# Hybrid attention layer: the smallest tile's top-k by striking out, causal products joined in and grouped, four banks for ten products, sparse PV in one piece

## The chip, the cores and the metric

The kernel runs on one core of a Trainium2 chip. The metric is the device time of one execution in microseconds (us). TensorE is the matrix engine (PE in the profile, with PEld for its weight loads), VectorE is DVE, ScalarE is ACT, GpSimd is POOL, SyncE is SP. A "bank" is one of the 512-column pieces of PSUM, the memory that TensorE writes its products to.

## What is computed

One layer with two attention branches over 16 meta tokens and 512 inputs (528 keys), 8 heads each, width 1024. Cut to what matters here:

```
proj = layer_norm(concat(meta, x)) @ w_in          # qa ka va ga qi ki wi cq ckv kpe gb
# latent branch: q from rms_norm(cq), k and v from rms_norm(ckv), 32 rotary columns, causal softmax
lb = (q_nope @ k_nope + q_pe @ k_pe) * scale_b;  lb = where(causal, lb, NEG);  ob = softmax(lb) @ vb
# sparse branch: an index score picks 128 keys for every query
idx = sum_h relu(qi_h @ ki) * wi_h
idx = where(s_pos < 16, inf, idx);  idx = where(causal, idx, -inf);  sel = top_k(idx, 128)
la = qa @ ka[sel] * scale_a + bias[t5_bucket(distance)];  oa = softmax(la) @ va[sel]
out = concat(oa * silu(ga), ob * silu(gb)) @ w_out;  return layer_norm(ALPHA * h + out)
```

The 16 meta keys are always picked, so the kernel has to find the 112 best of the others (`PICKED = 112`). A query in the first tile of 128 has only 128 others.

## The kernel before

**Tiling.** The 512 queries are four tiles of 128 (i = 0 to 3). Tile i sees `NK[i]` = 144, 272, 400 or 528 keys. Its index scores lie in `iw` in 128 (i + 1) columns. Those of future keys hold -1e38 (`FUTURE`).

**Order.** One list, `ORDER`, is built by `schedule()`. Every engine walks through it and issues what is its own of each stage, so the order on each engine follows the list and engines meet at semaphores. The list's stages that matter here:

- `("J", kind, n, m)`: a product ("job") of TensorE with three passes for each block of weights (high and low parts), which ACT, DVE or both copy out of its bank. Kinds: `gate` (n = 7 is the last), `uv` (values of the latent branch, five row chunks m), `qn`, `kn` (queries, keys of the latent branch for a pair of heads), `va`, `qa`, `ka` (the sparse branch), `out`, and `tq`, three transposes.
- `("TOPK", round, half)`: top-k on DVE. A round is one MAX8 (the 8 largest of a row) and one MATCH_REPLACE8 (these 8 set to `TAKEN`) for each tile; half 0 is tile 3, half 1 tiles 0, 1, 2. There are 14 rounds (`PICKED // 8`), so 28 halves. `pick(n)` puts the next n halves in the list. `MASK` then turns `iw` into the mask.
- `("S", g)`: scores of head g (0 to 7 latent, 8 to 15 sparse), `X` their exponentials on ACT, `R` the reciprocals and the scaling on POOL, `TP` the transposes into the two banks `ps_t`, `("PV", pair, part)` the products with the values for a pair of heads, in `ps_o`: part 0 is key chunk 0 (512 columns for each of two heads), part 1 the four others.
- `QPE`: ACT issues two DMAs that bring a pair's 32 rotary rows into `q_b`; the scores wait for them.

**Banks.** A job j before the last sixteen output products writes bank `j % 2` of `ps_j`. Its first matmul waits until job j - 2 is copied out, by ACT (`job_act`) and, where DVE copies, by DVE (`job_dve`):

```
                    elif j >= 2:
                        pe.wait_ge(job_act, BY_ACT[j - 1])
```

The two banks of `ps_t` hold index scores of odd heads until the last DVE addition (`i_add`), and the transposes from `TP` 0 on.

**The stretch around the last gate.** After the index scores TensorE makes `gate` 6, `uv` 0 and 1, `gate` 7, `uv` 2 and 3, `qn` 0, `kn` 0 (two halves), `uv` 4, `va` 0 (its first chunk) and then the scores of head 0. DVE meanwhile runs seven halves of top-k, copies `qn` 0 (L1001) and both halves of `kn` 0 (L1005), and goes on with three more halves.

**Scores of the latent branch.** For each tile there is one matmul in 4-byte floats (two for tile 3, which crosses a bank), which the trace records as two passes each (L1429), and behind it one bf16 matmul of 144 columns that adds the causal mask through the identity (L1433). Tiles 3, 1, 0 are unit 0, tile 2 is unit 1, and each unit has one semaphore.

**Sparse PV.** For pairs whose PV is `late` (g = 7, 9, 11, 13: four times) part 0 stands ahead of the last job of the stage, and part 1 behind `TP` and `tq`.

## Time and profile before

| | |
|---|---|
| median of 3 runs (lowest to highest) | 351.72 us (350.32 to 351.91) |
| the profiled execution's own time | 351.87 us |
| its span in the trace | 350.0 us |
| TensorE's mean granted clock | 0.992 of 2.4 GHz |
| busy: PE, PEld, DVE, ACT, POOL | 328.1, 272.5, 229.8, 171.9, 184.6 us |

The profile is of one execution. Its span is 1.9 us shorter than that execution's own time. Busy time of an engine is a sum over stages with different limits; matmul ends are modelled, so the starts of neighbouring rows tell more than their durations.

### The profile page before, as it was taken

Reading aid. Unit: us, or ns where it says so; the run is one execution under the profiler, and the core shown is the slowest. Engines: PE = TensorE matmul, PEld = TensorE weight load, DVE = VectorE, ACT = ScalarE, POOL = GpSimd, SP = SyncE. Lnnn points to the kernel's source line nnn. Section 1 sums busy time; section 2 is a strip of 40 time slices with the busy share of each in tenths; the row PEclk is TensorE's granted clock in tenths of the full one; section 3 lists DMA queues with packets and bytes.
Section 4 is the critical chain, followed back from the end, with each engine's and each line's share of the span. In section 5 each row is a group of like instructions: output and inputs, shape, how many; then the busy total and the mean of one; then the engine's idle time right before and its main releaser. Section 6 shows DMA issues by size and latency. Waiting matters only on the chain.

```text
span 350.0 us, 6150 instructions
## 1 busy us (share of the span) xinstructions
PE 328.1 (94%) x2147; PEld 272.5 (78%) x2147; DVE 229.8 (66%) x619; ACT 171.9 (49%) x378; POOL 184.6 (53%) x171
## 2 busy tenths in 40 slices
PE   0699999999999998999999999999999999999990
PEld 0488977788778776888696878788878888998990
DVE  5762220259965899987985985546676865644586
ACT  4664554353442444465443563747767762732211
POOL 4341899959322251354522459397838372460462
PEclk9999999999999999999999999999999999999996
DMA  7464333229422130101400114042323101130023
GB/s 265 172 179 175 120 122 122 90 65 298 143 81 84 60 113 24 62 15 63 136 2 15 62 28 187 11 143 91 93 91 95 61 10 53 60 123 0 2 89 153
DMA packets 11566, 32.87 MB, mean 94 GB/s; under 512 B 2392, under 2 KB 2392, under 8 KB 11536
## 3 DMA queue, kind: packets, MB, share of 16 engines
q1 hardware_dynamic: 8944, 27.08, 22.6%
q10 hardware_dynamic: 2592, 5.40, 5.1%
q8 instruction: 18, 0.29, 0.3%
q14 instruction: 12, 0.10, 0.1%
HBM read 29.83 MB, written 4.81 MB: 99 GB/s over the span
## 4 chain that ended last, share of the span: by engine, by line
PE 80%; DVE 12%; issue 3%; ACT 2%; DMA 2%; SPq 0%; DVEq 0%; ACTq 0%
PE ps_j L1233 47%; PE ps_o L1478 6%; PE ps_s L1429 6%; PE ps_s L1437 3%; PE ps_t L1233 2%; PE ps_j L1275 2%; PE ps_t L1448 2%; DVE iw L1071 2%; DMA res<-in_x 2%; PE ps_s L1399 2%; DVE top L1067 2%; PE ps_t L1453 1%; DVE iw L1055 1%; PE ps_j L1286 1%; PE ps_j L1291 1%
## 5 line engine op out<-in xcount | busy, mean ns | idle before, releaser
L537 POOL TENSOR_TENSOR wl<-raw,wh 128x1024 fp32r<-128x1024 f32 (+2 forms) x33 | 77.3, 2350 | 75.2 <-ACT wh L544 75.1
L1233 PE MATMUL ps_j<-hh,wh 128*128 128x512 f32 (+2 forms) x224 | 79.2, 354 | 0.1
L1233 PE MATMUL ps_j<-hl,wh 128*128 128x512 f32 (+2 forms) x224 | 78.0, 348 | 0.0
L1233 PE MATMUL ps_j<-hh,wl 128*128 128x512 f32 (+2 forms) x224 | 77.7, 347 | 0.0
L667 POOL TENSOR_SCALAR pr<-pr,rden 128x528 f32<-128x528 f32 (+1 forms) x64 | 35.1, 568 | 53.2 <-DVE rden L1113 53.2
L1233 PEld LDWEIGHTS ps_j<-hh,wh 128*128 128x128 f32 (+1 forms) x224 | 41.8, 187 | 10.1 <-issue 4.4
L1233 PEld LDWEIGHTS ps_j<-hh,wl 128*128 128x128 f32 (+1 forms) x224 | 41.8, 187 | 5.5
L1233 PEld LDWEIGHTS ps_j<-hl,wh 128*128 128x128 f32 (+1 forms) x224 | 41.8, 187 | 5.4 <-issue 0.2
L544 ACT ACTIVATE wh<-raw 128x1024 fp32r<-128x1024 f32 (+2 forms) x35 | 36.0, 1040 | 0.2 <-DMA raw<-in_weights 0.2
L1071 DVE MATCH_REPLACE8 iw<-top,iw 128x512 f32<-128x512 f32 (+3 forms) x56 | 26.2, 475 | 0.0
L677 POOL TENSOR_TENSOR bm<-bias,mask 128x144 f32<-128x144 f32 (+3 forms) x32 | 25.4, 827 | 0.0
L1067 DVE MAX8 top<-iw 128x8 f32<-128x512 f32 (+3 forms) x56 | 24.5, 478 | 0.0
L860 ACT ACTIVATE pr<-ps_s,mn 128x528 f32<-128x528 f32 (+3 forms) x32 | 16.9, 539 | 15.0 <-DVE mn L1099 15.0
L1233 PE MATMUL ps_j<-wh,hh 128*128 128x256 f32 (+1 forms) x80 | 22.9, 286 | 0.0
L1233 PE MATMUL ps_j<-wl,hh 128*128 128x256 f32 (+1 forms) x80 | 22.5, 281 | 0.0
L1233 PE MATMUL ps_j<-wh,hl 128*128 128x256 f32 (+1 forms) x80 | 22.4, 280 | 0.0
L1429 PE MATMUL ps_s<-k_b,q_b 96*128 96x240 f32 (+4 forms) x80 | 22.3, 406 | 0.0
L763 ACT ACTIVATE mix<-ps_j 128x512 f32<-128x512 f32 x8 | 4.8, 598 | 33.7 <-PE ps_j L1233 33.7
L860 ACT ACTIVATE pr<-pr,mn 128x528 f32<-128x528 f32 (+3 forms) x32 | 18.0, 567 | 3.5 <-DVE mn L1101 3.4
L1011 DVE TENSOR_TENSOR ks<-ps_j,ks 64x264 fp32r<-64x264 f32 x32 | 13.8, 430 | 8.9 <-ACT ks L793 8.1
L1233 PE MATMUL ps_j<-wh,mbh 128*128 128x256 f32 x64 | 18.5, 288 | 0.3 <-DVE res L1020 0.3
L1233 PE MATMUL ps_j<-wh,mbl 128*128 128x256 f32 x64 | 18.1, 283 | 0.0
(234 smaller groups left out, 785.6 us busy)
## 6 DMA issues: line engine op xcount, KB each, us to landing
raw<-in_weights SPq DMA_DIRECT2D x37, 512.0 KB, 3.4
bias_by_distance<-bias_vector ACTq DMA_DIRECT2D x1, 2624.0 KB, 13.4
bias<-bias_by_distance ACTq DMA_DIRECT2D x8, 264.0 KB, 3.4
res<-in_x SPq DMA_DIRECT2D x4, 512.0 KB, 5.4
out<-res SPq DMA_DIRECT2D x3, 512.0 KB, 2.6
pt<-in_ln_emb_g SPq DMA_DIRECT2D x1, 512.0 KB, 4.8
pt<-in_ln_emb_b SPq DMA_DIRECT2D x1, 512.0 KB, 6.8
q_b<-qpe ACTq DMA_DIRECT2D x8, 64.0 KB, 2.0
```

Source lines behind the costliest of these rows:

```text
L537: eng.tensor_tensor(ring_of(False, b), raw_of(b), ring_of(True, b).bitcast(F32), ALU.subtract).then_inc(done, 1)
L544: act.activation(ring_of(True, b), raw_of(b), ACT.Copy).then_inc(w_high, 1)
L667: pool.tensor_scalar(a, a, rden[:, k, n:n + 1], 1.0, ALU.mult, ALU.mult).then_inc(scaled, 1)
L677: pool.tensor_tensor(bm[:, h % 2, s], bias[:, h % 4, T - NK[i]:T], mask[:, s], ALU.add).then_inc(folded, 1)
L860: act.activation(dst, src, ACT.Exp, bias=mn[:, k, n:n + 1], scale=-1.0, accum_out=den[:, k, n:n + 1]).then_inc(e_done, 1)
L1011: dve.tensor_tensor(ks[HD - HD * v:P - HD * v, e, v, s], bank[HD * e:HD * e + HD, 0:264], ks[HD * v:HD * v + HD, e, v, s].bitcast(F32), AL ...
L1067: dve.max(top8[:, i, :], iw[:, IOFF[i]:IOFF[i] + P * (i + 1)]).then_inc(done, 1)
L1071: dve.match_replace(out=a, in_to_replace=top8[:, i, :], in_values=a, imm_value=TAKEN).then_inc(done, 1)
L1233: last = pe.matmul(dst, a, b, start=n == 0 and part[0], stop=n == count - 1 and part[1])
L1429: pe.matmul(dst, q_b[:, e, i * P:(i + 1) * P], k_b[:, e, a:b], start=True, stop=b <= c0)
L1437: last = pe.matmul(dst, qs[:, p % 2, e, i * P:(i + 1) * P], ks[:, e, v, a:b], start=v == 0, stop=v == 1)
L1478: last = pe.matmul(ps_o[HD * e:HD * e + HD, q0:NQ], v[0:r, j, c:c + HD], pt[0:r, e, CO[j]:CO[j] + NQ - q0], start=j == 0, stop=j == 4)
```

## The change

Five edits:

1. **Striking out.** A new stage `FLIP` writes the negated index scores of tile 0 in reverse column order into a tensor of its own, `drop`. Two rounds on `drop` take away the 16 lowest scores; rounds 3 to 14 leave tile 0 out. `MASK` reads `drop` backwards with the comparison turned round.
2. **Picks.** The pick ahead of `uv` 0 is 4 halves where it was 5, and the pick in stage g = 0 is 2 where it was 1.
3. **Four banks.** The ten jobs from `uv` 0 to `va` 0 (`FRONT`) rotate through four banks, two of `ps_j` and two of `ps_t`. Every job waits for the last job in its own bank (`PRIOR`), the first two in `ps_t` for `i_add`, and `TP` 0 for the last of `FRONT`. Outside `FRONT` the banks are those of before.
4. **Scores of the latent branch.** The causal matmuls stand behind all score matmuls of their unit: three in a row in unit 0, one in unit 1. Tiles 1 and 0 share their banks with the two pieces of tile 3 and start without the flag that begins a group.
5. **Sparse PV.** Both parts of a late pair stand together behind `TP` and `tq`.

```diff
@@ schedule()
     job("qpe", 1)
+    order.append(("FLIP",))
     pick(2)
     job("gate", 6, extra=0)
-    pick(5)
+    pick(4)
     job("uv", 0, 0, extra=0)
...
         if g < HEADS and g % 2 == 0:
-            pick(1 if g == 0 else 2)
+            pick(2)
...
         for n, j in enumerate(jobs):
-            if late and n == len(jobs) - 1:
-                order.append(("PV", pair, 0))
             job(*j, extra=int(j[0] == "out"))
...
         if late:
-            order.append(("PV", pair, 1))
+            order += [("PV", pair, 0), ("PV", pair, 1)]
@@ banks
+FRONT = range(NJ["uv", 0, 0], NJ["va", 0, 0] + 1)
+
+def bank_of(j):
+
+    if j in FRONT:
+        n = (0, 2, 3, 1)[(j - FRONT[0]) % 4]
+        return n if n >= 2 else (FRONT[0] + n) % 2
+    if j >= TAIL:
+        n = (j - TAIL) % 4
+        return n if n >= 2 else (TAIL + n) % 2
+    return j % 2
+
+BANK = [bank_of(j) for j in range(len(JOBS))]
+PRIOR = [max([i for i in range(j) if BANK[i] == BANK[j]], default=None) for j in range(len(JOBS))]
...
-TOPK_HALF = [(3,), (0, 1, 2)]
+DROP_ROUNDS = (P - PICKED) // 8
+TOPK_HALF = [lambda r: (3,), lambda r: (0, 1, 2) if r < DROP_ROUNDS else (1, 2)]
@@ build(), vector
+                elif stage == "FLIP":
+                    dve.wait_ge(i_add, 4 * HEADS)
+                    dve.tensor_scalar(drop_back, iw[:, IOFF[0]:IOFF[0] + P], -1.0, None, ALU.mult).then_inc(flipped, 1)
...
+                        a = iw[:, IOFF[i]:IOFF[i] + P * (i + 1)] if i else drop[:, :]
...
                         dve.tensor_scalar(mask[:, POFF[i] + META:POFF[i] + NK[i]],
-                                          iw[:, IOFF[i]:IOFF[i] + P * (i + 1)], TAKEN, MASKED, ALU.is_gt,
-                                          ALU.mult).then_inc(masked, 1)
+                                          iw[:, IOFF[i]:IOFF[i] + P * (i + 1)] if i else drop_back, TAKEN, MASKED,
+                                          ALU.is_gt if i else ALU.is_le, ALU.mult).then_inc(masked, 1)
@@ build(), tensor
+            def bank_free(j):
+
+                if PRIOR[j] is None and BANK[j] >= 2:
+                    pe.wait_ge(i_add, 4 * HEADS)
+                elif BANK[j] >= 2 and j >= TAIL > PRIOR[j]:
+                    pe.wait_ge(t_act, 2 * HEADS)
+                    pe.wait_ge(t_dve, 2 * HEADS)
+                elif PRIOR[j] is not None:
+                    pe.wait_ge(job_act, BY_ACT[PRIOR[j] + 1])
+                    if BY_DVE[PRIOR[j] + 1]:
+                        pe.wait_ge(job_dve, BY_DVE[PRIOR[j] + 1])
...
                                 if g < HEADS:
-                                    c0 = NK[i] - 144
-                                    pe.matmul(dst, q_b[:, e, i * P:(i + 1) * P], k_b[:, e, a:b], start=True,
-                                              stop=b <= c0)
-                                    if b > c0:
-                                        lo = max(a, c0)
-                                        last = pe.matmul(ps_s[:, SOFF[i] + lo:SOFF[i] + b], identb[:, :],
-                                                         causal[:, lo - c0:b - c0], start=False, stop=True)
+                                    pe.matmul(dst, q_b[:, e, i * P:(i + 1) * P], k_b[:, e, a:b], start=i >= 2,
+                                              stop=b <= NK[i] - 144, skip_group_check=True)
...
+                        if g < HEADS:
+                            for i in tiles:
+                                a = SOFF[i] + NK[i] - 144
+                                last = pe.matmul(ps_s[:, a:a + 144], identb[:, :], causal[:, :], start=False, stop=True,
+                                                 skip_group_check=True)
                         last.then_inc(s_mm, 1)
```

DVE from the third round of top-k to the copies of `qn` 0 and `kn` 0 (`q_b`, `k_b`), before and then of the change:

```order
L1067 MAX top<-iw 128x8 [waits topk_long]
L1071 MATCH_REPLACE iw<-top,iw 128x512 [waits topk_long]
L1067 MAX top<-iw 128x8 [waits topk_short] x3
L1071 MATCH_REPLACE iw<-top,iw 128x128 [waits topk_short]
L1071 MATCH_REPLACE iw<-top,iw 128x256 [waits topk_short]
L1071 MATCH_REPLACE iw<-top,iw 128x384 [waits topk_short]
L1067 MAX top<-iw 128x8 [waits topk_long]
L1071 MATCH_REPLACE iw<-top,iw 128x512 [waits topk_long]
L1001 TENSOR_SCALAR q_b<-ps_j 64x512 [waits job_mm]
L1005 COPY k_b<-ps_j 64x264 [waits job_mm] x2
```

```order
L1092 MAX top<-iw 128x8 [waits topk_long]
L1096 MATCH_REPLACE iw<-top,iw 128x512 [waits topk_long]
L1092 MAX top<-iw 128x8 [waits topk_short] x2
L1096 MATCH_REPLACE iw<-top,iw 128x256 [waits topk_short]
L1096 MATCH_REPLACE iw<-top,iw 128x384 [waits topk_short]
L1020 TENSOR_SCALAR q_b<-ps_t 64x512 [waits job_mm]
L1024 COPY k_b<-ps_t 64x264 [waits job_mm]
L1024 COPY k_b<-ps_j 64x264 [waits job_mm]
L1092 MAX top<-iw 128x8 [waits topk_long]
L1096 MATCH_REPLACE iw<-top,iw 128x512 [waits topk_long]
```

The third round has two tiles in its second half, and the fourth half of tile 3 stands behind the copies; the first two rounds, ahead of this piece, are as long as before, with `FLIP` ahead of them.

TensorE in the same stretch, from `kn` 0 (its two halves) over `uv` 4 to the first matmul of `va` 0, before and then of the change; `ps_j` and `ps_t` tell the bank:

```order
L1233 MATMUL ps_j<-ckh,wh 128x264 [waits job_act,job_dve,w_low,w_high]
L1233 MATMUL ps_j<-ckl,wh 128x264
L1233 MATMUL ps_j<-ckh,wl 128x264
L1233 MATMUL ps_j<-ckh,wh 128x264 [waits job_act,job_dve,w_low,w_high]
L1233 MATMUL ps_j<-ckl,wh 128x264
L1233 MATMUL ps_j<-ckh,wl 128x264
L1233 MATMUL ps_j<-wh,ckh 16x512 [waits job_act,job_dve,w_low,w_high]
L1233 MATMUL ps_j<-wh,ckl 16x512
L1233 MATMUL ps_j<-wl,ckh 16x512
L1233 MATMUL ps_j<-wh,hh 128x256 [waits job_act,job_dve,w_low,w_high]
```

```order
L1258 MATMUL ps_t<-ckh,wh 128x264 [waits job_act,job_dve,w_low,w_high]
L1258 MATMUL ps_t<-ckl,wh 128x264
L1258 MATMUL ps_t<-ckh,wl 128x264
L1258 MATMUL ps_j<-ckh,wh 128x264 [waits job_act,job_dve,w_low,w_high]
L1258 MATMUL ps_j<-ckl,wh 128x264
L1258 MATMUL ps_j<-ckh,wl 128x264
L1258 MATMUL ps_j<-wh,ckh 16x512 [waits job_act,job_dve,w_low,w_high]
L1258 MATMUL ps_j<-wh,ckl 16x512
L1258 MATMUL ps_j<-wl,ckh 16x512
L1258 MATMUL ps_t<-wh,hh 128x256 [waits job_act,job_dve,w_low,w_high]
```

The order is the same. The second half of `kn` 0 waited for the copy of `qn` 0, two jobs back, and now waits for that of `uv` 2, four jobs back; `va` 0 is now the one that waits for the copy of `qn` 0.

TensorE in the scores of a latent head, before and then of the change:

```order
L1429 MATMUL ps_s<-k_b,q_b 128x240 [waits kp,qpe_in,i_add,job_dve,job_act]
L1429 MATMUL ps_s<-k_b,q_b 128x288
L1433 MATMUL ps_s<-causal,identb 128x144
L1429 MATMUL ps_s<-k_b,q_b 128x272
L1433 MATMUL ps_s<-causal,identb 128x144
L1429 MATMUL ps_s<-k_b,q_b 128x144
L1433 MATMUL ps_s<-causal,identb 128x144
L1429 MATMUL ps_s<-k_b,q_b 128x400 [waits i_add]
L1433 MATMUL ps_s<-causal,identb 128x144
```

```order
L1455 MATMUL ps_s<-k_b,q_b 128x240 [waits kp,qpe_in,i_add,job_dve,job_act]
L1455 MATMUL ps_s<-k_b,q_b 128x288
L1455 MATMUL ps_s<-k_b,q_b 128x272
L1455 MATMUL ps_s<-k_b,q_b 128x144
L1464 MATMUL ps_s<-causal,identb 128x144 x3
L1455 MATMUL ps_s<-k_b,q_b 128x400 [waits i_add]
L1464 MATMUL ps_s<-causal,identb 128x144
```

The matmuls are the same nine; two of the three places where a bf16 matmul stood between two 4-byte ones inside unit 0 are gone.

## Rows read from the trace of the kernel before

**Rows 1.** The page: busy time, share of the span, instructions of TensorE; weights made by ACT.

```profile
PE 328.1 (94%) x2147; PEld 272.5 (78%) x2147; DVE 229.8 (66%) x619; ACT 171.9 (49%) x378; POOL 184.6 (53%) x171
...
L544 ACT ACTIVATE wh<-raw 128x1024 fp32r<-128x1024 f32 (+2 forms) x35 | 36.0, 1040 | 0.2 <-DMA raw<-in_weights 0.2
```

**Rows 2.** Busy time in 120 to 140 us, all engines, clock, DMA.

```profile
120.00:140.00 20.00, 18.01 (x91) 13.65 (x90) 19.32 (x65) 9.77 (x15) 6.20 (x11) 1.00 0.26 85
```

**Rows 3.** TensorE in order of time, 120 to 135 us: start, duration, line, shape.

```profile
120.62 0.40 PE L1233 MATMUL ps_j<-wh,ckl 128*128 128x512 f32 x1
120.86 0.40 PE L1233 MATMUL ps_j<-wl,ckh 128*128 128x512 f32 x1
121.44 0.47 PE L1233 MATMUL ps_j<-wh,ckh 128*128 128x512 f32 x1 [0.18 <-ACT mix L763]
121.75 0.40 PE L1233 MATMUL ps_j<-wh,ckl 128*128 128x512 f32 x1
...
131.23 0.28 PE L1233 MATMUL ps_j<-ckh,wl 128*128 128x264 f32 x1
133.13 0.36 PE L1233 MATMUL ps_j<-ckh,wh 128*128 128x264 f32 x1 [1.62 <-DVE q_b L1001]
...
134.04 0.40 PE L1233 MATMUL ps_j<-wl,ckh 128*16 128x512 f32 x1
134.41 0.35 PE L1233 MATMUL ps_j<-wh,hh 128*128 128x256 f32 x1
```

**Rows 4.** DVE in order of time, 120 to 133 us.

```profile
120.14 0.69 DVE L1067 MAX8 top<-iw 128x8 f32<-128x512 f32 x1
...
121.53 1.07 DVE L1067 MAX8 top<-iw 128x8 f32<-128x128 f32 x3
122.52 0.07 DVE L1071 MATCH_VALUE_LOAD iw<-top,iw 128x8 f32 x1
...
122.77 0.08 DVE L1071 MATCH_VALUE_LOAD iw<-top,iw 128x8 f32 x1
...
132.30 0.69 DVE L1001 TENSOR_SCALAR q_b<-ps_j 64x512 f32<-64x512 f32 x1
```

**Rows 5.** Rotary DMAs of head 0: issue, landing of all eight, load for first scores.

```profile
134.49 1.22 ACTq L802 DMA_DIRECT2D q_b<-qpe  x2
...
DMA to landing us min/median/max: 1.9/2.0/3.7
...
137.31 0.30 PEld L1429 LDWEIGHTS ps_s<-k_b,q_b 96*128 96x128 f32 x2
```

**Rows 6.** TensorE in the scores of head 5, and causal weight loads of all heads.

```profile
181.53 1.05 PE L1429 MATMUL ps_s<-k_b,q_b 96*128 96x240 f32 x4
182.42 0.23 PE L1433 MATMUL ps_s<-causal,identb 128*128 128x144 bf16 x1
...
183.06 0.46 PE L1429 MATMUL ps_s<-k_b,q_b 96*128 96x144 f32 x2
183.35 0.23 PE L1433 MATMUL ps_s<-causal,identb 128*128 128x144 bf16 x1
183.42 0.88 PE L1429 MATMUL ps_s<-k_b,q_b 96*128 96x400 f32 x2
...
L1433 PEld LDWEIGHTS ps_s<-causal,identb 128*128 128x128 bf16 x32 | 3.1, 98 | 1.9
```

**Rows 7.** Chain that ended last, by start and duration, 232 to 298 us.

```profile
232.38 2.91 PE ps_j L1233 x24
235.29 1.01 PE ps_o L1478 x4
236.30 3.12 PE ps_j L1233 x24
...
240.87 1.75 PE ps_o L1478 x16
...
295.81 2.60 PE ps_o L1478 x20
```

More of the change, by code:

```diff
@@ L300, with topk_count @@
 LAST_IN_JOB = max(n for n, j in enumerate(JOBS) if j[0] not in ("out", "tq"))
-TOPK_HALF = [(3,), (0, 1, 2)]
+DROP_ROUNDS = (P - PICKED) // 8
+TOPK_HALF = [lambda r: (3,), lambda r: (0, 1, 2) if r < DROP_ROUNDS else (1, 2)]
+def topk_count(r, half):
+    return 2 * sum(len(TOPK_HALF[half](n)) for n in range(r))
 def build(nc, x, meta, ln_emb_g, ln_emb_b, rel_bias, ln_post_g, ln_post_b, weights, gains, onehot, cos_t,
@@ L340, in build @@
         wi = sb("wi", [P, QT, HEADS])
+        drop = sb("drop", [P, P])
         top8 = sb("top8", [P, QT, 8])
@@ L466, in build @@
         centred = sem("centred")
+        flipped = sem("flipped")
         squared = sem("squared")
@@ L481, in job_bank @@
         def job_bank(j):
-            if tail_bank(j) in (2, 3):
-                return ps_t[:, 512 * tail_bank(j) - 1024:512 * tail_bank(j) - 512]
-            return ps_j[:, (TAIL + tail_bank(j)) % 2 if j >= TAIL else j % 2, :]
+            if BANK[j] >= 2:
+                return ps_t[:, 512 * BANK[j] - 1024:512 * BANK[j] - 512]
+            return ps_j[:, BANK[j], :]
         def vec_bank(n):
@@ L1060, in _ @@
                     r, half = arg
-                    tiles, done = TOPK_HALF[half], topk[half]
+                    tiles, done = TOPK_HALF[half](r), topk[half]
                     if r == 0:
                         dve.wait_ge(i_add, 4 * HEADS)
+                        dve.wait_ge(flipped, 1)
                     for n, i in enumerate(tiles):
+                        a = iw[:, IOFF[i]:IOFF[i] + P * (i + 1)] if i else drop[:, :]
                         if r:
-                            dve.wait_ge(done, len(tiles) * (2 * r - 1) + n + 1)
-                        dve.max(top8[:, i, :], iw[:, IOFF[i]:IOFF[i] + P * (i + 1)]).then_inc(done, 1)
+                            last = TOPK_HALF[half](r - 1)
+                            dve.wait_ge(done, topk_count(r, half) - len(last) + last.index(i) + 1)
+                        dve.max(top8[:, i, :], a).then_inc(done, 1)
                     for n, i in enumerate(tiles):
-                        a = iw[:, IOFF[i]:IOFF[i] + P * (i + 1)]
-                        dve.wait_ge(done, len(tiles) * 2 * r + n + 1)
+                        a = iw[:, IOFF[i]:IOFF[i] + P * (i + 1)] if i else drop[:, :]
+                        dve.wait_ge(done, topk_count(r, half) + n + 1)
                         dve.match_replace(out=a, in_to_replace=top8[:, i, :], in_values=a,
@@ L1074, in _ @@
                     for half in range(2):
-                        dve.wait_ge(topk[half], 2 * len(TOPK_HALF[half]) * ROUNDS)
+                        dve.wait_ge(topk[half], topk_count(ROUNDS, half))
                     for i in range(QT):
                         dve.tensor_scalar(mask[:, POFF[i] + META:POFF[i] + NK[i]],
-                                          iw[:, IOFF[i]:IOFF[i] + P * (i + 1)], TAKEN, MASKED, ALU.is_gt,
-                                          ALU.mult).then_inc(masked, 1)
+                                          iw[:, IOFF[i]:IOFF[i] + P * (i + 1)] if i else drop_back, TAKEN, MASKED,
+                                          ALU.is_gt if i else ALU.is_le, ALU.mult).then_inc(masked, 1)
                     dve.wait_ge(masked, QT)
@@ L1262, in _ @@
                     low_made(pe, NB["out", n])
[L1263 to L1264 removed]
+                    bank_free(j)
                     output_part(n, 0, 0, 3)
@@ L1446, in _ @@
                         pe.wait_ge(t_act, g)
+                    else:
+                        pe.wait_ge(job_act, BY_ACT[FRONT[-1] + 1])
+                        pe.wait_ge(job_dve, BY_DVE[FRONT[-1] + 1])
                     for i in range(QT):
```

18 lines of the change are left out of this document (3 added, 15 removed).

## The prediction

> **What bounds the kernel now.** I read the page first, for which engine is full. TensorE is busy 94% of the span, the next engine 66% [rows 1]. So only two things can shorten this program: taking idle time away from TensorE, or taking work away from it. I then looked for where TensorE is not full, in the table by stretches. It is idle for 22 us in all (350.0 less 328.1), most of them ahead of the first products and behind the last ones, which the change doesn't touch. Of the stretches in between, 120 to 140 us loses most: TensorE has 18.01 of 20 us there, and DVE 19.32 [rows 2]. TensorE's order of time in that stretch shows four gaps [rows 3]. The reader should look at the distance between starts, not at the idle time in brackets, because the modelled ends overlap. Last I read the two places where TensorE changes from one kind of work to another: the scores of a latent head [rows 6] and the late PV [rows 7].
>
> **Four banks and striking out: the gaps.** Two 512-column products in a row start 0.24 us apart (120.62, 120.86). The next starts 0.58 us later, so 0.34 is lost, and the one after it is 0.31 behind instead of 0.24, another 0.07 [rows 3]. That is 0.41 us for `uv` 1, which waits for the copy of `gate` 6 out of the bank two jobs back. The same gap stands once more, at `uv` 3: two, 0.82 us. The third is the big one. The second half of `kn` 0 starts 1.90 us after the last matmul of the first; 264 columns at that rate take 0.12, so 1.78 is lost, and 0.07 behind it, 1.85. Its releaser is DVE's copy of `qn` 0. The fourth, ahead of `va` 0, is 0.37 less 0.24 and 0.07, 0.20 us. Sum of all four: 2.87 us.
>
> With four banks `uv` 1 and `gate` 7 need only the last index addition, long done, and `uv` 3 waits for `uv` 0. `kn` 0 waits for `gate` 7 and `uv` 2. So the first three gaps go. What waits now for the copy of `qn` 0 is `va` 0, and this is where the top-k edit matters. TensorE would reach it at 134.41 - 2.87 = 131.54.
>
> When is that copy made? Before, DVE goes from 120.14 to 132.30, three rounds and one more half of tile 3 in 12.16 us [rows 4]. A half of tile 3 is 121.53 - 120.14 = 1.39, so a round is 3.59. Tile 0's part of a round: its value load and replacement take 122.77 - 122.52 = 0.25, and its MAX8 some 0.20 of the 0.99 that three take for 128, 256 and 384 columns (by columns alone a sixth, 0.17). So 0.45 us a round, 12 rounds of them saved, 5.4 us of DVE in all. Of these only one falls ahead of the copy, and the moved half counts more. After: `FLIP`, two whole rounds 7.18, one half of 1.39, one of 3.59 - 1.39 - 0.45 = 1.75. `FLIP` isn't in the trace. Its nearest rows are 128 columns of MAX8 by share, 0.17, below, and the 512-column copy of `q_b`, 0.69, above [rows 4]; I take 0.25, what value load and replacement of the same 128 columns need. The copy starts at 120.14 + 0.25 + 7.18 + 1.39 + 1.75 = 130.71 and ends at 131.40. TensorE started 0.14 after it before (132.99 to 133.13), so `va` 0 may start at 131.54: exactly when TensorE gets there. The gaps are all gone, with nothing to spare: at a `FLIP` of 0.69 us, 0.44 comes back.
>
> **What is late next.** Behind `va` 0 come the first scores. They need the rotary rows of head 0, whose two DMAs ACT issues at 134.49 in 1.22 us together, when `uv` 4 is done. The second goes off near 135.1 and lands a median 2.0 us later, at 137.1; the first load for the scores is at 137.31 [rows 5]. The distance from `uv` 4 to the scores shrinks by the fourth gap, 0.20, so the load would be due at 137.11 on the old clock and waits some 0.1 us. If it lands after 3.7 us, the longest of the eight, the wait is 1.7. I take 0.1. Front: 2.87 - 0.1 = 2.8 us. From there everything, weight loading too, moves up with TensorE; ACT waited for raw weights 0.2 us in the whole program [rows 1], so I charge nothing for them, and at most that if their cover goes.
>
> The rest of the saved DVE time lies beside a full TensorE and is worth nothing.
>
> **Scores of the latent heads.** 528 columns in 4-byte floats take 182.42 - 181.53 = 0.89 us, 1.69 ns a column; 144 would take 0.24 but take 183.35 - 183.06 = 0.29 behind a causal product. The causal product itself holds the array for 0.07 (183.35 to 183.42) [rows 6]. So each change back from bf16 to 4-byte costs about 0.05, three inside a head's scores. Grouping leaves one: 0.10 saved. Against that, the second and third causal product in a row can no longer hide their weight load behind a long matmul. The record of such a load is 98 ns [rows 6]. If it sets the pace, each costs 0.03 more, 0.06, and 0.04 is left; if it is hidden too, 0.10. I take the middle, 0.07, times 8 heads: 0.56 us, between 0.3 and 0.8. If load and product follow each other with no overlap, it is 2 x 0.10 - 0.10 = 0.10 lost a head, 0.8 us in all. Leaving out the flag that begins a group on tiles 1 and 0 costs nothing: same matmuls, same columns.
>
> A rule of the Trainium skill speaks against this edit. "TensorE: Matmul & The Clock Gate", section on LDWEIGHTS, gives a load of 128 columns 107 ns whatever the contraction, and its section on back-to-back gaps some 81 ns for a load and a 128-column product in a stream. By the first, grouping would be worth about 0.03 a head, 0.2 us in all; by the second about 0.08, 0.6 us. The case's row has 98 ns for the load and no two causal products in a row.
>
> **Sparse PV in one piece.** In the chain the first part takes 1.01 us and the second 1.75; in one piece ten matmuls of the same kind take 2.60. The job between the parts takes 3.12 where its twin takes 2.91, because TensorE has to come back to it [rows 7]. So 1.01 + 1.75 + 0.21 - 2.60 = 0.37 us, four times: 1.5 us. The end of the PV stays where it was against the next scores, so ACT's and DVE's copies behind it see the same distance, and the copies of the last `ka` get 1 us more before the scores that need them. `TP` comes 1.2 us earlier; it needs POOL's scaling, and POOL is busy 53% [rows 1]. At the least, if the 0.21 is paid somewhere in any case, it is 1.01 + 1.75 - 2.60 = 0.16, four times: 0.6 us. I take the 1.5, since the twin job shows the 0.21 gone where no PV stands ahead of it.
>
> **Sum.** 2.8 + 0.56 + 1.5 = 4.8 us off the profiled execution's own 351.87 gives 347.0. The median shown is 0.15 below that execution, so 346.9 to 347.0; I give 347.0.
>
> **The rivals.**
> - *The rotary DMA takes the place of the wait.* For: it lands some 0.2 us ahead now, and one of eight took 3.7. Against: the median of the eight is 2.0. Time 347.0 + 1.6 = 348.6. Chance 0.10.
> - *The grouped loads are laid bare.* For: nothing long covers the second and third. Against: loads here overlap matmuls everywhere. 347.0 + 0.56 + 0.8 = 348.4. Chance 0.08. The 107 ns of the Trainium skill's page named above would lie between this and my sum.
> - *DVE stays late.* Reading or writing columns backwards is not in the trace. If DVE makes the copy of `qn` 0 at 132.30 as before, `va` 0 starts at 133.13 and 1.6 us of the gaps come back: 348.6. Chance 0.08.
> - *Slower: the same mechanism, larger.* Each microsecond of `FLIP` above 0.25 stands on the path. From 4.8 + 1.8 = 6.6 us on, the kernel is slower by over 0.5%; at 7 us it ends at 353.8. It would take 27 times my price; no DVE row of 128 columns comes near. Chance 0.03.
> - *No change.* TensorE arrives earlier everywhere and waits there for weights or for exponentials instead, or the waits on four banks do not open: 351.5. Against: 0.2 us of waiting for raw weights in the whole program [rows 1], and stretches that are full of TensorE work. Chance 0.06.
>
> **How the numbers follow.** The forecast has 0.65, between 345.7 and 348.2: 0.3 for the flip and the loads, the lower PV bound of 0.6, and below the lowest of the three runs, which is 1.4 under the median. The first three rivals, 0.26, end by 348.6. The range of 345.7 to 349.2 leaves out the last two and some of the tails. A measurement here can tell about 0.5% (1.8 us) from no change. Faster by over that: the forecast and three rivals, 0.91; within: 0.06; slower: 0.03.
>
> **What the new profile would show.** No gap ahead of `uv` 1, `uv` 3 and the second half of `kn` 0, and `va` 0 starting near 131.5; DVE's copy of `qn` 0 starting near 130.7 and `FLIP` at 0.2 to 0.3 us; the first scores near 134.5, with a wait of some 0.1 for the DMA; causal products in a row 0.07 to 0.10 apart and a head's scores shorter by 0.04 to 0.10; the late PV at 2.6 us in one piece. The prediction is wrong if `va` 0 or the first scores wait by more than half a microsecond, or if TensorE has new gaps behind 140 us.

## The result, and the profile after

| | before | after |
|---|---|---|
| median (lowest to highest) | 351.9 us of 6 runs (350.32 to 352.14) | 345.93 us of 6 runs (345.44 to 346.59) |
| the profiled execution's own time, its span | 351.87, 350.0 us | 346.34, 344.5 us |
| TensorE's mean granted clock | 0.992 | 0.994 |

The ratio is 0.9838, 95% interval 0.9817 to 0.9858: 1.6% faster, 5.7 us of 351.9 (the two medians lie 6.0 apart). The page's first rows, which answer to [rows 1], say that TensorE is still the full engine, and that DVE lost 35 instructions and 4.3 us of work:

```profile
PE 325.1 (94%) x2147; PEld 273.5 (79%) x2147; DVE 225.5 (65%) x584; ACT 171.7 (50%) x378; POOL 184.8 (54%) x171
```

**How much of it is the change.** The two programs are the same up to `FLIP`, yet in these two executions the one after is 0.53 us ahead at one and the same index product of TensorE (the last with 384 columns into `ps_t` ahead of 80 us; 78.15 us before, 77.62 after), and 0.56 is there at 14 us already (14.07 and 13.51 for the same transposes), behind an input DMA that landed sooner. That is the start of one execution and not the change: over the fourteen traces of this case this product starts between 75.64 and 78.15 us. So I count from it and call it the mark. To the end of the span it is 271.83 us before and 266.91 after: 4.92 us. The prediction's sum was 4.8.

**The stretch that was short of TensorE.** The table by stretches for 120 to 140 us, against [rows 2] (there 18.01 of 20 us at TensorE, 19.32 at DVE):

```profile
120.00:140.00 20.00, 20.00 (x115) 16.85 (x115) 19.77 (x61) 12.22 (x24) 7.73 (x12) 1.00 0.29 93
```

TensorE in order of time, from the first half of `kn` 0 to head 0's scores, against [rows 3]:

```profile
129.58 0.28 PE L1258 MATMUL ps_t<-ckh,wh 128*128 128x264 f32 x1
...
129.82 0.28 PE L1258 MATMUL ps_t<-ckh,wl 128*128 128x264 f32 x1
129.94 0.28 PE L1258 MATMUL ps_j<-ckh,wh 128*128 128x264 f32 x1
...
130.78 0.39 PE L1258 MATMUL ps_j<-wl,ckh 128*16 128x512 f32 x1
131.07 0.36 PE L1258 MATMUL ps_t<-wh,hh 128*128 128x256 f32 x1
...
133.87 0.28 PE L1258 MATMUL ps_t<-wl,hh 128*128 128x256 f32 x1
134.08 1.83 PE L1455 MATMUL ps_s<-k_b,q_b 96*128 96x240 f32 x8
```

The second half of `kn` 0 now starts 0.12 us behind the last matmul of the first, where it was 1.90. `va` 0 starts 0.29 behind `uv` 4's last matmul instead of 0.37; 0.24 of that is the matmul itself. Its second matmul is again 0.07 late (131.07 to 131.26, not in the lines), so 0.12 is left of this gap's 0.20. The scores start 0.21 behind `va` 0's last, where 0.12 is its 256 columns: the wait of 0.1 us for the rotary rows. They start at 134.08 against 137.34; less the 0.53 of the mark that is 2.7 us.

DVE in the same stretch, against [rows 4]:

```profile
119.57 0.22 DVE L1049 TENSOR_SCALAR drop<-iw 128x128 f32<-128x128 f32 x1
119.90 0.69 DVE L1092 MAX8 top<-iw 128x8 f32<-128x512 f32 x1
...
129.65 0.54 DVE L1096 MATCH_REPLACE8 iw<-top,iw 128x384 f32<-128x384 f32 x1
130.23 0.69 DVE L1020 TENSOR_SCALAR q_b<-ps_t 64x512 f32<-64x512 f32 x1
```

`FLIP` takes 0.22 us, with its columns written in reverse order. From its start to the copy of `qn` 0 are 10.66 us; the prediction had 10.57 (120.14 to 130.71).

**Latent scores.** Head 5 in TensorE's order of time, against [rows 6]:

```profile
177.70 1.76 PE L1455 MATMUL ps_s<-k_b,q_b 96*128 96x240 f32 x8
179.30 0.35 PE L1464 MATMUL ps_s<-causal,identb 128*128 128x144 bf16 x3
179.49 0.88 PE L1455 MATMUL ps_s<-k_b,q_b 96*128 96x400 f32 x2
```

From the head's first matmul to tile 2's it is 1.79 us; before it was 183.42 - 181.53 = 1.89. The three causal products together hold TensorE for 0.19 us (179.30 to 179.49).

**Late PV.** The chain that ended last, 215 to 240 us, against [rows 7]:

```profile
227.84 5.86 PE ps_j L1258 x48
...
235.16 2.60 PE ps_o L1508 x20
```

PV is one piece of 2.60 us where two of 1.01 and 1.75 stood. The two jobs ahead of it take 5.86 us, 2.91 + 3.12 before. Per late PV that is 0.16 + 0.17 = 0.33 us.

**What is late now.** TensorE still has three waits of over 0.25 us behind 140 us. The first, with what ACT and DVE do ahead of it (`v_a` takes the copy of a `va` product; `mn` are the minima of a head's rows, which DVE finds and the exponentials need):

```profile
146.34 0.28 PE L1258 MATMUL ps_j<-wl,hh 128*128 128x256 f32 x1
147.06 0.36 PE L1258 MATMUL ps_j<-ckh,wh 128*128 128x264 f32 x1 [0.43 <-ACT v_a L800]
```

```profile
144.13 0.70 ACT L879 ACTIVATE pr<-ps_s,mn 128x528 f32<-128x528 f32 x1 [3.95 <-DVE mn L1124]
...
146.21 0.59 ACT L789 ACTIVATE q_b<-ps_j 64x512 f32<-64x512 f32 x1
146.69 0.38 ACT L800 ACTIVATE v_a<-ps_j 128x256 f32<-128x256 f32 x1
```

```profile
142.38 0.54 DVE L1096 MATCH_REPLACE8 iw<-top,iw 128x384 f32<-128x384 f32 x1
142.84 1.74 DVE L1124 TENSOR_REDUCE mn<-ps_s 128x1 f32<-128x528 f32 x4
```

Read it from below: DVE comes to head 1's minima only when its top-k halves are done; ACT's exponentials, 3.95 us idle, wait for them; ACT's share of the copy of `qn` 1 is queued behind the exponentials; and `kn` 1 needs that copy's bank. The bracket names `v_a`, but the copy that frees this bank is that of `q_b`, which ended at 146.80; the start is 0.26 behind it. The kernel before had a gap here too, ahead of the second half of `kn` 1:

```profile
150.26 0.29 PE L1233 MATMUL ps_j<-ckh,wl 128*128 128x264 f32 x1
150.93 0.37 PE L1233 MATMUL ps_j<-ckh,wh 128*128 128x264 f32 x1 [0.38 <-ACT v_a L781]
```

The two are alike in size, 0.55 us lost before and 0.60 after, but they are different waits. Before, ACT had been done with `qn` 1 in time and sat idle until TensorE had made the `va` product that `v_a` copies:

```profile
149.10 0.59 ACT L770 ACTIVATE q_b<-ps_j 64x512 f32<-64x512 f32 x1
150.20 0.38 ACT L781 ACTIVATE v_a<-ps_j 128x256 f32<-128x256 f32 x1 [0.52 <-PE ps_j L1233]
```

The copy of `qn` 1 ended at 149.68 and the first half of `kn` 1 started at 150.00, 0.32 behind it, where TensorE needs some 0.25. So the wait that comes last in the kernel after was 0.07 us from showing. The other two, behind the matmuls at 187.57 (0.47 lost, ahead of the second half of `kn` 3) and 307.23 us (0.43, ahead of an output product, behind DVE's `MIX`), stood in the profile before too, behind those at 191.54 and 312.73 us with 0.47 and 0.42.

### The profile page after: what moved, and what is told of

Same layout as the page of the kernel before. It is cut to its first block, busy times and chain, and to the rows that moved or that the text cites. A ratio compares the mean times of both kernels' runs of the same rounds, so it can differ in the third digit from the quotient of the medians.

```text
span 344.5 us, 6116 instructions
## 1 busy us (share of the span) xinstructions
PE 325.1 (94%) x2147; PEld 273.5 (79%) x2147; DVE 225.5 (65%) x584; ACT 171.7 (50%) x378; POOL 184.8 (54%) x171
## 4 chain that ended last, share of the span: by engine, by line
PE 82%; DVE 10%; issue 3%; ACT 2%; DMA 1%; DVEq 0%; ACTq 0%; SPq 0%
PE ps_j L1258 48%; PE ps_o L1508 6%; PE ps_t L1258 6%; PE ps_s L1455 5%; PE ps_s L1459 3%; PE ps_j L1310 2%; PE ps_t L1478 2%; PE ps_s L1426 2%; PE ps_t L1483 2%; DVE iw L1077 1%; DMA res<-in_x 1%; PE ps_j L1330 1%; PE ps_j L1321 1%; PE ps_j L1326 1%; DVE tmp L1053 1%
## 5 line engine op out<-in xcount | busy, mean ns | idle before, releaser
L1258 PE MATMUL ps_j<-hh,wh 128*128 128x512 f32 (+2 forms) x216 | 75.6, 350 | 0.1
L1258 PE MATMUL ps_j<-hl,wh 128*128 128x512 f32 (+2 forms) x216 | 74.7, 346 | 0.0
L1258 PE MATMUL ps_j<-hh,wl 128*128 128x512 f32 (+2 forms) x216 | 74.5, 345 | 0.0
L1258 PEld LDWEIGHTS ps_j<-hh,wh 128*128 128x128 f32 (+1 forms) x216 | 40.3, 186 | 6.4 <-issue 1.0
L1258 PEld LDWEIGHTS ps_j<-hh,wl 128*128 128x128 f32 (+1 forms) x216 | 40.3, 187 | 5.1
L1096 DVE MATCH_REPLACE8 iw<-top,iw 128x512 f32<-128x512 f32 (+2 forms) x42 | 22.6, 542 | 0.0
L1092 DVE MAX8 top<-iw 128x8 f32<-128x512 f32 (+2 forms) x42 | 21.8, 547 | 0.1
L1258 PE MATMUL ps_j<-wh,hh 128*128 128x256 f32 (+1 forms) x72 | 20.5, 285 | 0.0
L1258 PE MATMUL ps_j<-wl,hh 128*128 128x256 f32 (+1 forms) x72 | 20.2, 280 | 0.0
L1258 PE MATMUL ps_j<-wh,hl 128*128 128x256 f32 (+1 forms) x72 | 20.1, 280 | 0.0
```

The lines of the kernel that those rows point to most:

```text
L1092: dve.max(top8[:, i, :], a).then_inc(done, 1)
L1096: dve.match_replace(out=a, in_to_replace=top8[:, i, :], in_values=a, imm_value=TAKEN).then_inc(done, 1)
L1258: last = pe.matmul(dst, a, b, start=n == 0 and part[0], stop=n == count - 1 and part[1])
```

## The experiments

Lost time in a gap is always the distance of two starts less that of two neighbours of the same kind. "To scores" and "to end" in the table are the start of head 0's scores and the end of the span, counted from the mark, in one profiled execution. The ratios and their intervals are of the runs, each against those of the kernel before beside it. "The kernel after" is the changed kernel. The median of the kernel before was 351.13 (21 runs) beside the first four, 351.16 (21) beside the next four and 350.79 (11) beside the last four.

| kernel | median us (runs) | ratio to before, 95% | to scores | to end |
|---|---|---|---|---|
| before | | 1 | 59.20 | 271.83 |
| after | 345.93 (6) | 0.9838, 0.9817 to 0.9858 | 56.45 | 266.91 |
| front_only | 348.20 (6) | 0.9912, 0.9887 to 0.9937 | 56.45 | 269.06 |
| group_only | 350.28 (12) | 0.9975, 0.9961 to 0.9990 | 59.15 | 270.97 |
| pv_only | 350.25 (10) | 0.9966, 0.9950 to 0.9983 | 60.68 | 271.77 |
| keys_apart | 349.12 (6) | 0.9938, 0.9916 to 0.9959 | 56.44 | 270.38 |
| banks_only | 350.28 (12) | 0.9979, 0.9962 to 0.9997 | 57.84 | 271.23 |
| strike_only | 349.52 (10) | 0.9955, 0.9941 to 0.9969 | 58.06 | 270.61 |
| four_flips | 346.32 (6) | 0.9875, 0.9852 to 0.9899 | 57.17 | 267.68 |
| spare_bank | 345.21 (5) | 0.9846, 0.9822 to 0.9870 | 56.49 | 266.50 |
| tile0_kept | 346.67 (6) | 0.9880, 0.9859 to 0.9902 | 56.46 | 268.10 |
| late_pick | 346.26 (4) | 0.9866, 0.9849 to 0.9883 | 56.49 | 267.01 |
| mix_later | 345.80 (4) | 0.9857, 0.9838 to 0.9876 | 56.45 | 266.46 |
| best | 344.68 (5) | 0.9829, 0.9810 to 0.9847 | 56.49 | 265.40 |

### The three parts, one at a time

**front_only** keeps `FLIP`, the picks and the four banks, and has the causal products and PV of before (shortened; against the kernel after):

```diff
+            if late and n == len(jobs) - 1:
+                order.append(("PV", pair, 0))
...
-            order += [("PV", pair, 0), ("PV", pair, 1)]
+            order.append(("PV", pair, 1))
...
+                                    if b > c0:
+                                        lo = max(a, c0)
+                                        last = pe.matmul(ps_s[:, SOFF[i] + lo:SOFF[i] + b], identb[:, :],
...
```

> The kernel before with the striking out, the moved picks and the four banks, but with the causal products one by one and the late PV in two parts. My theory, that the gaps around the last gate are worth what the two traces show between 120 and 137 us: 2.7 us less than before, 349.2 on a before of 351.9. Rival, that part of the gain seen in the traces came with the 0.6 us by which the first products started earlier in the one profiled execution and belongs to this edit: 3.3 us less.

Measured: 2.75 us up to the scores, 2.77 to the end; 0.88% by the ratio.

**group_only** is the kernel before with the causal products behind the score matmuls of their unit, and nothing else of the change (shortened; against the kernel before):

```diff
+                            for i in tiles:
+                                a = SOFF[i] + NK[i] - 144
+                                last = pe.matmul(ps_s[:, a:a + 144], identb[:, :], causal[:, :], start=False, stop=True,
...
```

> The kernel before with the causal products of a unit grouped and joined in, nothing else. My theory as predicted: 0.07 us a head, 0.6 us less in all. Theory after reading the trace of the changed kernel, where a head's scores are 0.11 shorter: 0.9 us less. Rival, that the shorter scores only bring the wait for the exponentials of the head before nearer: under 0.3 us less.

Measured: 0.25%. From the first to the last latent head's scores and on to the first sparse head's it is 84.23 us (143.38 - 59.15) where before it is 144.27 - 59.20 = 85.07: 0.84 us in eight heads, 0.105 a head.

**pv_only** is the kernel before with both parts of a late PV together (against the kernel before):

```diff
-            if late and n == len(jobs) - 1:
-                order.append(("PV", pair, 0))
...
-            order.append(("PV", pair, 1))
+            order += [("PV", pair, 0), ("PV", pair, 1)]
```

> The kernel before with both parts of a late PV together, nothing else. My theory: 0.37 us for each of four, 1.5 us less. Theory after reading the trace of the changed kernel, where three of the four give 0.31 each: 1.3 us less. Rival, that the earlier transposes wait for the scaling or that the products behind wait for it: under 0.6 us less.

Measured: 0.34%. Its profiled execution lost 1.5 us between the mark and head 0's scores, in code that is the same. From 132.7 to 136.0 us TensorE's granted clock is 0.50 (the third number from the end), its lower level of 1.2 GHz:

```profile
132.70:136.00 3.30, 3.30 (x18) 3.30 (x17) 3.27 (x13) 0.34 (x1) 0.00 (x0) 0.50 0.16 40
```

`va` 0's products of 256 columns start 0.21 us apart there and 0.12 behind it. Until 131.10, some 1.5 us ahead of the fall, TensorE had sat idle for 1.61 us, for the copy of `qn` 0; the trace of the kernel before has that wait too (1.62) and no fall. So only the distances behind the scores of head 6 are read. From these to those of head 8 it is 0.37 us less, and 0.32 less in each of the three stretches that hold another late PV: 1.33 us.

Together, 2.77 + 0.84 + 1.33 = 4.94 us against 4.92 in the kernel after. The parts add up, so none of them can stand in another's wait by more than the noise of these counts.

The fall of the clock in pv_only says one thing more. The change takes the wait of 1.8 us away, and this wait can cost a fall as well, 1.5 us where it came. How often it does in the kernel before isn't shown: its one trace has none. Of its 21 runs beside the second four kernels, 8 have a mean granted clock of 0.988 and a median of 351.79 us, and the 7 from 0.995 up have 350.39, but where their clock fell was not recorded. The counts from the mark leave this out, and the medians may hold some of it.

### Within the front: banks and striking out

**banks_only** has the four banks, and top-k and picks as before; **strike_only** has `FLIP` and the picks, and two banks. Both have the causal products and PV of before. The lines below are from strike_only, against the kernel after, shortened:

```diff
 def bank_of(j):
 
-    if j in FRONT:
-        n = (0, 2, 3, 1)[(j - FRONT[0]) % 4]
-        return n if n >= 2 else (FRONT[0] + n) % 2
...
```

> The kernel before with the four banks alone; top-k and picks as before. My theory, that banks and top-k each open only part of the gaps: the gaps ahead of the products uv 1, uv 3 and of the second half of kn 0 go, but DVE copies qn 0 at 132.3 as before, so va 0 starts some 133.1 on the clock of before, 1.3 us earlier. DVE's three halves of top-k behind it still hold up the minima of head 0, now by 0.8 us against TensorE, so the second head's scores wait: 0.5 us less than before in all. Rival, that the banks alone are the gain and the top-k edit adds nothing on the path: 2.7 us less.

> The kernel before with the striking out and the moved picks alone; two banks. My theory: the two small gaps stay, the copy of qn 0 starts when the product is done, and the gap ahead of the second half of kn 0 shrinks from 1.9 to 0.8 us: 1.1 us less than before. Rival, that top-k alone is the gain: 2.7 us less. If both theories of parts hold, this and the banks alone sum to 1.6 of the 2.7 us that they give together.

Measured: banks alone reach the scores 1.36 us earlier, but only 0.60 of it is left at the end. TensorE's order of time, groups that waited:

```profile
131.45 0.36 PE L1258 MATMUL ps_t<-wh,hh 128*128 128x256 f32 x1 [1.40 <-DVE q_b L1021]
...
140.73 1.16 PE L1456 MATMUL ps_s<-k_b,q_b 96*128 96x240 f32 x4 [0.67 <-ACT pr L880]
```

The short gaps are gone, and the long one stands ahead of `va` 0: a bank more doesn't make the copy of `qn` 0 come sooner. Then DVE, with a half of tile 3 more ahead of the copy and tile 0 in every round, comes late to head 0's minima (137.74 us), the exponentials are late, and head 1's scores wait 0.83 us for the bank of head 0's: a gap that neither the kernel before nor the one after has. Striking out alone makes the copy sooner and keeps the short gaps; the second half of `kn` 0 loses 0.67 instead of 1.78:

```profile
130.17 0.28 PE L1257 MATMUL ps_j<-ckh,wl 128*128 128x264 f32 x1
130.96 0.36 PE L1257 MATMUL ps_j<-ckh,wh 128*128 128x264 f32 x1 [0.52 <-DVE q_b L1019]
```

It reaches the scores 1.14 us earlier and ends 1.22 earlier. Up to the scores the two nearly add: 1.36 + 1.14 = 2.50 of the 2.75 that they give together. At the end they give 0.60 and 1.22 alone and 2.77 together. Most of what is missing, 0.75, is the new wait of banks_only: head 1's scores are 6.39 us behind head 0's there, and 5.64 before.

**four_flips** does `FLIP` four times, with the same values, to price its place on the path:

```diff
-                    dve.tensor_scalar(drop_back, iw[:, IOFF[0]:IOFF[0] + P], -1.0, None, ALU.mult).then_inc(flipped, 1)
+                    for n in range(4):
+                        if n:
+                            dve.wait_ge(flipped, n)
+                        dve.tensor_scalar(drop_back, iw[:, IOFF[0]:IOFF[0] + P], -1.0, None, ALU.mult).then_inc(flipped, 1)
```

> The changed kernel with the flip made four times instead of once, so 1.0 us more of DVE ahead of the copy of qn 0. My theory, that va 0 waits for this copy with no slack to spare: 0.9 us more than the changed kernel, va 0 starting 0.9 later. Rival, that the copy has slack behind the four banks: 0.2 us or nothing more.

```profile
118.58 1.00 DVE L1052 TENSOR_SCALAR drop<-iw 128x128 f32<-128x128 f32 x4
```

```profile
129.79 0.39 PE L1261 MATMUL ps_j<-wl,ckh 128*16 128x512 f32 x1
130.85 0.36 PE L1261 MATMUL ps_t<-wh,hh 128*128 128x256 f32 x1 [0.67 <-DVE q_b L1020]
```

DVE works 1.00 - 0.22 = 0.78 us more (first fence), `va` 0 loses 0.83 instead of 0.06 (second), the scores come 0.72 later and the end 0.77. So there was nothing to spare ahead of `va` 0: over these 0.78 us, DVE's time there is the kernel's. This is the traces' answer; the interval of its ratio overlaps that of the kernel after.

### What the DVE time behind the copy is worth

The prediction called it worth nothing. **tile0_kept** gives it back: in every round from the fourth on, all of them behind the copy of `qn` 0, DVE does tile 0's MAX8 and MATCH_REPLACE8 again, and no result depends on what they write.

```diff
+                    if half and r > DROP_ROUNDS:
+                        dve.max(spare8[:, :], drop[:, :]).then_inc(kept, 1)
...
+                        dve.match_replace(out=iw[:, IOFF[0]:IOFF[0] + P], in_to_replace=spare8[:, :],
+                                          in_values=drop[:, :], imm_value=TAKEN).then_inc(kept, 1)
```

> The changed kernel with the MAX8 and the replacement of tile 0 put back in the eleven rounds behind the copy of qn 0, as work whose result nothing reads: 5 us more of DVE, none of it ahead of the copy. The prediction's theory, that DVE time saved behind the copy lies beside a full TensorE and is worth nothing: no difference from the changed kernel, 0.2 us at most. Rival, from the trace of the changed kernel, where the first key product of the second pair waits 0.6 us for a copy that ACT makes behind the exponentials of head 1, and these for DVE's minima: two of the rounds stand ahead of these minima, 0.9 us more.

The first of its eleven extra rounds starts at 131.78, behind the copy of `qn` 0, and `va` 0 and the scores are where they were (56.46 us). Three of them stand ahead of head 1's minima, and there it costs:

```profile
141.89 0.09 DVE L1106 MATCH_VALUE_LOAD iw<-spare,drop 128x8 f32 x1
141.96 0.28 DVE L1106 MATCH_REPLACE8 iw<-spare,drop 128x128 f32<-128x128 f32 x1
142.15 1.75 DVE L1134 TENSOR_REDUCE mn<-ps_s 128x1 f32<-128x528 f32 x4
```

```profile
144.46 0.28 PE L1268 MATMUL ps_j<-wl,hh 128*128 128x256 f32 x1
146.37 0.36 PE L1268 MATMUL ps_j<-ckh,wh 128*128 128x264 f32 x1 [1.63 <-ACT q_b L791]
```

Counted from the mark the minima start 1.29 us later than in the kernel after (142.15 - 75.64 against 142.84 - 77.62), `kn` 1 starts 1.29 later (its gap loses 1.79 instead of 0.60), and the end is 1.19 later. The eight rounds behind this point cost nothing that is seen. So 1.2 us of the change's gain are three saved rounds of tile 0 (3 x 0.45 = 1.35) behind the copy; the rival had two of them, 0.9 us.

### The gaps that are left

**keys_apart** makes the first half of `kn` ahead of `va`, so that the job two back from the second half, whose copy it waits for, is the first half and no longer `va`:

```diff
-            jobs = [("qn", p + 1)] + jobs + [("kn", p + 1, 0), ("kn", p + 1, 1)]
+            jobs = [("qn", p + 1), ("kn", p + 1, 0)] + jobs + [("kn", p + 1, 1)]
```

> The changed kernel with one more edit: in the stages of heads 1 and 5 a value product stands between the two key products, instead of ahead of both. The second key product there waits 0.6 and 0.5 us for the copy of the value product two jobs back. My theory, that a gap of this kind goes when the job two back is copied out earlier: 1.1 us less than the changed kernel, 344.9. Rival, that the keys are then late for the scores or the value product waits in its place: no difference.

```profile
146.89 0.36 PE L1258 MATMUL ps_j<-wh,hh 128*128 128x256 f32 x1 [2.91 <-ACT q_b L789]
```

A miss: 3.5 us slower than the kernel after. Now `va`, the next to use `qn` 1's bank, comes to it sooner and waits for the same ACT copy, 3.07 us; from the mark it starts at 69.42, where `kn` 1 started at 69.44 in the kernel after (146.89 - 77.47, 147.06 - 77.62). The wait is set by when ACT gets past the exponentials, not by which job asks.

The longer wait is 3.07 - 0.60 = 2.47 us of the loss. Another 1.5 is the clock: 1.4 us behind the end of the wait, from 148.3 to 151.7 us, TensorE runs at 1.2 GHz (granted 0.50), and products of 256 columns start 0.21 us apart instead of 0.12:

```profile
148.30:151.70 3.40, 3.40 (x19) 3.40 (x18) 0.00 (x0) 0.39 (x1) 0.52 (x1) 0.50 0.00 0
```

```profile
148.62 0.42 PE L1258 MATMUL ps_j<-wh,hl 128*128 128x256 f32 x1
148.84 0.42 PE L1258 MATMUL ps_j<-wl,hh 128*128 128x256 f32 x1
```

Head 2's scores come 3.99 us later than in the kernel after, counted from the mark. All six runs have a mean granted clock of 0.987 or 0.988, where the kernel after has 0.992 to 0.994. The other half of the theory came true: the gap ahead of the second half of `kn` 3 is gone, and 0.50 us comes back between the scores of heads 5 and 6.

**spare_bank** gives the second half of `kn` 1 and `kn` 3 a bank that is idle then, one of `ps_o`:

```diff
+SPARE = {NJ["kn", 1, 1]: 0, NJ["kn", 3, 1]: 2}
...
+    if j in SPARE:
+        return 4
```

> The changed kernel with the second key product of the second and fourth pair written to the bank of the PV products (ps_o), which is idle then, so that it need not wait for the copy of the value product two jobs back. The run with the value product between the two key products lost 3 us, since the value product then stood right behind the query product and waited for its copy, which ACT makes behind four exponentials. My theory, that the long value product must stay where it is and only the short product needs another bank: both gaps of 0.6 us go, 1.1 us less than the changed kernel. Rival, that the next job waits in its place: no difference.

Measured: the gap near 188 us is gone, 0.41 us at the end; the one near 146 stays, since there it is the first half that waits. **late_pick** moves one half of top-k from head 0 behind head 1's minima:

```diff
-            pick(2)
+            pick({0: 1, 2: 3}.get(g, 2))
```

> The changed kernel with one of the two halves picked in the stage of head 0 moved to that of head 2. Takes 1.4 us of DVE from ahead of the minima of head 1. My theory: the first key product of the second pair no longer waits for its copy, but the second one then waits for that of the value product as in the kernel before; 0.1 us less than the changed kernel. Rival, that the wait was all of that gap: 0.6 us less.

```profile
141.26 1.75 DVE L1124 TENSOR_REDUCE mn<-ps_s 128x1 f32<-128x528 f32 x4 [0.37 <-PE ps_s L1464]
```

```profile
146.37 0.28 PE L1258 MATMUL ps_j<-ckh,wl 128*128 128x264 f32 x1
146.97 0.36 PE L1258 MATMUL ps_j<-ckh,wh 128*128 128x264 f32 x1 [0.31 <-ACT v_a L800]
```

Counted from the mark the minima start 1.2 us earlier, now released by TensorE, and the first half of `kn` 1 waits no more; but the second then waits for `v_a`, and the end is 0.1 us later. The two edits each take one of two waits that stand in a row. **mix_later** puts `MIX` 2 behind one more output product:

```diff
-    order += [("TP", 2 * HEADS - 1), ("J", "tq", 2 * HEADS - 1, 0), ("MIX", 2)]
+    order += [("TP", 2 * HEADS - 1), ("J", "tq", 2 * HEADS - 1, 0)]
+    job("out", *outs.pop(0))
+    order.append(("MIX", 2))
```

> The changed kernel with the last but one casting of the mix put one output product later in the order. DVE's subtraction of 1.5 us then no longer stands ahead of the copy that the third of the last output products waits for. My theory: the gap of 0.55 us at 307.8 goes, 0.5 us less than the changed kernel. Rival, that the wait moves to the next product: no difference.

Measured: the gap near 307 us is gone, 0.45 us at the end. **best** is these three edits together.

> The changed kernel with the spare bank for two key products, the later pick and the later casting together. My theory: three gaps of 0.6, 0.55 and 0.55 us go, 1.7 us less than the changed kernel. The spare bank alone lost only the gap of the fourth pair, since the first key product of the second pair waited in place of the second. Rival, that each edit's gain is taken by the next wait: 0.6 us less, as with the spare bank alone.

```profile
145.69 0.28 PE L1267 MATMUL ps_j<-wl,hh 128*128 128x256 f32 x1
145.81 0.28 PE L1267 MATMUL ps_j<-ckh,wh 128*128 128x264 f32 x1
...
146.05 0.29 PE L1267 MATMUL ps_j<-ckh,wl 128*128 128x264 f32 x1
146.18 0.28 PE L1267 MATMUL ps_o<-ckh,wh 128*128 128x264 f32 x1
```

No wait is left there (all four starts follow each other at 0.12), nor near 188 and 307 us. The trace is 266.91 - 265.40 = 1.51 us shorter than that of the kernel after, and 0.60 + 0.47 + 0.43 = 1.50 was in the three gaps. The ratios to before are 0.9829 and 0.9838, their intervals overlap, and the two were not measured side by side. late_pick, within 0.1 us of the kernel after in the trace, was measured beside best: 346.26 (345.88 to 346.37) to 344.68 (344.13 to 345.34). That best is faster than the kernel after is shown by the traces and by this pair, not by the two ratios.

## Why the prediction came out right, point by point

- **Four banks and striking out, 2.87 less 0.1.** Right: 2.7 us at the scores, 2.75 and 2.77 in front_only. The first three gaps closed, and 0.12 of the fourth's 0.20 is left. The bracket at `uv` 3 (128.82 us before) names POOL's `wl`; it was the bank all the same, since the gap is gone in banks_only and stands in strike_only. That the copy and TensorE meet at `va` 0 "with nothing to spare" was right too: four_flips costs what it adds.
- **`FLIP` at 0.25.** 0.22 by its row, 0.33 with the empty time to the next instruction. The price of a round of tile 0 by columns, 0.45, held.
- **The rotary DMA.** 0.1 us, as worked out; ACT issued the two DMAs at 131.22 us and the eight of the program landed in a median of 2.0 us, as in [rows 5]. In four_flips, where `va` 0 comes later and the DMAs don't, the scores start 0.11 behind `va` 0's last matmul instead of 0.21. The rival of 1.6 to 1.7 didn't come.
- **Latent scores, 0.07 a head, 0.56 in all.** The mechanism was right and the size low: 0.10 a head from the rows of head 5, 0.84 in all in group_only, just outside the bounds of 0.3 to 0.8. The term that was mis-sized is the load of the grouped causal products, for which 0.03 each was set aside. The three hold TensorE for 0.19 us, 0.064 each, no more than the 0.07 of a single one. Their loads are hidden, and the whole 0.10 is kept. The Trainium skill's page "TensorE: Matmul & The Clock Gate" by its formula puts a load of 128 columns at an estimate of 107 ns (section "LDWEIGHTS (loading the stationary operand)"), and a load and a 128-column product in a stream at some 81 ns (section "Back-to-back issue gap"). Neither sets the pace of these three: 64 ns lies under both. The formula of the second section for the isolated gap, the columns at 2.4 GHz and 2.5 ns, gives an estimate of 62.5 ns for 144 columns, and with that the trace agrees.
- **Late PV, 0.37 each, 1.5 in all.** 0.33 each by the chain, 1.33 in pv_only. The 0.16 of the PV itself was exact; of the job's 0.21 only 0.17 came back: two jobs take 5.86 where twice the 2.91 would be 5.82.
- **"The rest of the saved DVE time lies beside a full TensorE and is worth nothing."** Wrong, and the step whose reason failed. Three of the later rounds, 1.3 us, stand ahead of head 1's minima, and tile0_kept shows them worth 1.2 us. I had moved everything behind the front up with TensorE. But DVE doesn't move up with it; it has a queue of its own, and it had to gain about as much as TensorE did. It nearly did: against the mark the minima came 2.35 us earlier and TensorE 2.7. Of the 2.35 some 1.35 are these rounds. The round saved ahead of the copy, less `FLIP`, gives 0.1, and most of the rest is idle time of DVE in the kernel before that has gone, 0.44 and 0.31 us:

```profile
133.78 0.43 DVE L1005 COPY k_b<-ps_j 64x264 f32<-64x264 f32 x1 [0.44 <-PE ps_j L1233]
143.49 0.16 DVE L1113 RECIPROCAL rden<-den 128x1 f32<-128x1 f32 x1 [0.31 <-ACT pr L860]
```

Without the three rounds the front would have been worth some 1.6 us, an estimate from 2.77 and tile0_kept's 1.19. The sum was right because the assumption (no new wait behind the front) held for a reason that it didn't name: that part of the number is luck.
- **"Wrong if TensorE has new gaps behind 140 us."** By this sign the prediction was wrong in this step, though the time doesn't show it: the wait of 0.60 us ahead of the first half of `kn` 1 is new, and it stands in place of the old 0.55 ahead of the second half. The trace of before had the warning, the 0.07 us by which the copy of `qn` 1 was in time. The prediction didn't look there.
- **Why 345.93 and not 347.0.** The profiled execution came out at 346.34: of the 0.7 us less than forecast, 0.53 is the start of the program, which is not the change, and 0.12 the sum. The other 0.4 is the median, which lies below this execution. The forecast took off its 4.8 us from one trace whose mark, 78.15 us, is the latest of the fourteen.

## What to carry to other kernels

When a front is moved up, list every queue that feeds what stands behind it and ask whether it moves up as well; time saved on an engine "beside the full one" is what keeps the next wait shut. Fixing one of two causes (a bank too few, a copy too late) can be worth much less than its share: the banks alone gained 1.36 us at the scores and kept 0.60 at the end, since DVE, not relieved, was late behind them; with both edits what was gained at the scores, 2.75, stayed. When a wait is a bank's, giving the job another bank removes it only if no job next to it needs the same engine's copy, so look for the second wait in the row before pricing the first. When a wait of TensorE grows, read its granted clock behind it: in keys_apart 1.5 us of the loss was there and not in the wait.

## What was not expected of the hardware

- Three bf16 products of 144 columns, each with its own weight load, run 0.064 us apart in a row; the record of the load is 97 ns, so loads and products overlap even there. By the rows of head 5 a change from bf16 back to 4-byte floats costs about 0.05 us (144 columns take 0.29 where 0.24 would be their rate). Grouping took away two of them and saved 0.105 a head.
- DVE writing a row of 128 columns backwards takes 0.22 us, and four in a row 1.00: no dearer than the 0.27 to 0.28 that a replacement in 128 columns takes. The same write forwards was not measured.
- In the middle of the program TensorE's granted clock falls to 1.2 GHz in two traces, each time some 1.5 us after a wait: of 2.91 us idle in keys_apart and of 1.61 in pv_only. Behind 1.62 us idle in the kernel before and 1.63 in tile0_kept it didn't fall.
- TensorE starts 0.25 to 0.26 us behind the end of the ACT copy for which it waits (146.80 to 147.06 in the kernel after; in late_pick, spare_bank, tile0_kept and keys_apart 0.25 each; 0.34 once, in the kernel before, 150.59 to 150.93), and 0.14 to 0.15 behind DVE's (five kernels). A row's bracket may name a later copy of the same engine that ends at that time: the bank's owner and this distance tell which it was.
